# Rotary embedding: the halves of each head exchanged by transfers in SBUF instead of permutation products

## The chip, the cores and the metric

One core of a Trainium2 chip. The metric is the device time of one execution in microseconds; a kernel's time is the median of its runs. TensorE, VectorE, ScalarE and GpSimd run side by side, each with its own stream of instructions, and wait for each other on semaphores; the transfers are issued from SyncE's and ScalarE's streams.

## The reference

One inference step of a two-layer encoder trunk over 512 prompt tokens and 64 sample tokens, handled together as 576 columns. Each layer has three token mixers fed by one projection (an mLSTM with 4 heads of 128, a gated MLP, a sliding-window attention with 8 query heads and 2 key heads of 64), a gated merge, an output projection and a SwiGLU network. The part that matters here is the rotary embedding of the attention's queries and keys:

```python
def rope(x, pos):
    half = x.shape[-1] // 2
    ...
    x1, x2 = xf[..., :half], xf[..., half:]
    return jnp.concatenate([x1 * cos - x2 * sin, x1 * sin + x2 * cos], axis=-1).astype(x.dtype)
```

Every feature of a head needs, beside itself, the feature 32 places on or back in the same head.

## The kernel before

Activations lie with features on the partitions and the 576 tokens along them. Weights stream in chunks of 128 output features (1024 x 128, 512 KB). For each chunk SyncE loads a raw buffer, GpSimd splits it in two operations (L747 makes the high part, L750 the low part, both 128x1024, reading the raw buffer and another tile in SBUF), and TensorE makes 48 products of 288 columns (L799, function `feature_group`, called by `main`). Mostly two pairs of split buffers are in use, so the split of a chunk waits until TensorE has ended the chunk two before it (semaphore chunk_used), and TensorE waits for the split of its own (chunk_split). ScalarE copies each finished chunk out of PSUM (`tile`, L1630).

PSUM is four units of 1024 columns. Every result has its place in one written-out list, `MIX` among others, and takes the unit of its place modulo 4; it waits until the unit's former holder, four places before, has been read (`empty`, `read`).

The order of TensorE's work around the change is written out by hand. The four query chunks wq0 to wq3 (to the tile `wq`) and the chunks su0 to su3 are put between the steps of the mLSTM's heads h = 0 to 3: `scores(h)`, `outputs(h)` and `back(h)` (transposes, L1208 and L1209). The keys' chunk wk went to the tile `kall` (KA is one half of it) long before. Then come su1, back(3), the rotary products of the keys (`rope(4)`) and of query tile 0, su2, those of tiles 1 and 2, su3, that of tile 3, the key transposes ko (L1289, L1290), the chunk sv0, and the first score products of the attention (`sw_scores(0)`, L1308). These wait for all five rotations (rope_ready) and for a copy of the keys with their two heads exchanged (kx_moved), which ScalarE issues as two transfers within SBUF behind the first rotation. Three more chunks sv1 to sv3 alternate with the attention's steps.

A rotary product (L1274) multiplies a tile of 128 features (two heads of 64) by the permutation matrix `perm` from the constants, in two halves of 288 columns, into one PSUM unit r0 to r4. VectorE then rotates: for the keys and the four query tiles in turn, `rope(i)` makes tile x cos, unit x sin, and writes the sum over the tile. All of VectorE's two-operand operations are recorded under L1910. Before this VectorE ends the mLSTM's last head: `gate_head(3)` (L2302), ScalarE's y_hi (L1681), and `y_lo(3)`.

On ScalarE the copies of wq0 to wq3 stand between the heads' steps: `head_hi(h)` writes y_hi, `decay(h)` the exponentials with which VectorE's `weigh_scores(h)` makes the operand of `outputs(h)`. The tile `mid` holds the mLSTM's queries of head h in its slice h and the keys in slice 4 + h; these are last read by the products of `scores(h)`, whose last unit is a3_h. Slices 6 and 7 later take the layer norm's parameters (`LNG`, `LNB`).

Of the kernel before, what the change touches and what calls it, by code (L numbers as in the profile page):

```python
# [16 lines left out]
T = SEQ + DSEQ  # L17
# [20 lines left out]
for _n, _w in (("ident", 128), ("mneg", 128), ("ones", 128), ("perm", 128), ("cos", T),  # L38
               ("sin", T), ("m1", 256), ("sel", 512)):
    CO[_n] = (_at, _at + _w)  # L40
    _at += _w
NCONST, NFIRST = _at, CO["perm"][0]


def constants():
# [3 lines left out]
    def put(n, a):  # L49
        c[:a.shape[0], CO[n][0]:CO[n][1]] = a  # L50
    p = np.arange(128)
    put("ident", np.eye(128, dtype=np.float32))
    swap = np.where(p % 64 < 32, p + 32, p - 32)
    perm = np.zeros((128, 128), np.float32)
    perm[swap, p] = 1.0
    put("perm", perm)
# [87 lines left out]
def swa_slot(i):  # L144
# [8 lines left out]
    + ["r4", "r0", "su2", "r1", "r2", "su3", "r3", "ko"]  # L153
# [131 lines left out]
def build(nc, A, O):  # L285
# [4 lines left out]
    with ctx:  # L290
# [146 lines left out]
        kx_moved, out_done = sem("kx_moved"), sem("out_done")  # L437
        dve_step, act_step = sem("dve_step"), sem("act_step")
# [322 lines left out]
        def _(pe):  # L761
# [15 lines left out]
            for l in range(DEPTH):  # L777
# [483 lines left out]
                def rope(i):  # L1261

                    nm = f"r{i}"
                    pe.wait_ge(unit_of(l, nm), empty(l, nm))
                    if i == 4:
                        if apart(l, "wk", nm):
                            pe.wait_ge(unit_of(l, "wk"), read(l, "wk"))
                        src = KA[:, 0:T]
                    else:
                        if apart(l, f"wq{i}", nm):  # L1270
                            pe.wait_ge(unit_of(l, f"wq{i}"), read(l, f"wq{i}"))
                        src = WQ[:, i, :]
                    for h in range(2):
                        m = pe.matmul(halves(l, nm)[:, h, :], K_["perm"], src[:, h * HALF:(h + 1) * HALF],  # L1274
                                      start=True, stop=True)
                    m.then_inc(done_by(nm), 1)

                main("su1", P_SU + 1)
                back(3)
                rope(4)  # L1280
                rope(0)
                main("su2", P_SU + 2)
                rope(1)
                rope(2)
                main("su3", P_SU + 3)
                rope(3)
# [185 lines left out]
        def _(act):  # L1472
# [19 lines left out]
            for l in range(DEPTH):  # L1492
# [193 lines left out]

                tile("mo0", MO[:, 0, :], ACT.Tanh, 0.5)
# [11 lines left out]
                tile("wq1", WQ[:, 1, :])  # L1699
                head_hi(1)  # L1700
                decay(2)
                tile("wq2", WQ[:, 2, :])
                tile("wq3", WQ[:, 3, :])
                head_hi(2)
                decay(3)
# [4 lines left out]
                act.wait_ge(unit_of(l, _a(3)[2]), read(l, _a(3)[2]))  # L1710
# [894 lines left out]
```

## Time and profile before

| | us |
|---|---|
| median of 3 runs | 2123.87 (2123.57 to 2126.81) |
| the profiled execution | 2126.99 |
| its span, first to last instruction | 2125.2 |
| TensorE busy | 2092.9 (98%) |
| GpSimd busy | 1216.3 (57%) |
| VectorE busy | 696.2 (33%) |
| ScalarE busy | 409.2 (19%) |

Times within the trace are counted from the span's start. Busy time of TensorE includes products that overlap, so the chain of waits, which follows the work back from the end, tells better what an instruction costs on the path. Each product in f32 with plain operands is recorded as two instructions.

### The profile page before, as it was taken

Reading aid. Unit: us, or ns where it says so; the run is one execution under the profiler, and the core shown is the slowest. Engines: PE = TensorE matmul, PEld = TensorE weight load, DVE = VectorE, ACT = ScalarE, POOL = GpSimd, SP = SyncE. Lnnn points to the kernel's source line nnn. Section 1 sums busy time; section 2 is a strip of 40 time slices with the busy share of each in tenths; the row PEclk is TensorE's granted clock in tenths of the full one; section 3 lists DMA queues with packets and bytes.
Section 4 is the critical chain, followed back from the end, with each engine's and each line's share of the span. In section 5 each row is a group of like instructions: output and inputs, shape, how many; then the busy total and the mean of one; then the engine's idle time right before and its main releaser. Section 6 shows DMA issues by size and latency. Waiting matters only on the chain.

```text
span 2125.2 us, 37767 instructions
## 1 busy us (share of the span) xinstructions
PE 2092.9 (98%) x16679; PEld 2021.3 (95%) x16679; DVE 696.2 (33%) x1223; ACT 409.2 (19%) x906; POOL 1216.3 (57%) x596
## 2 busy tenths in 40 slices
PE   7999999999999999999999999999999999999997
PEld 6999898999999999999999989899999999999997
DVE  5223466331345110011464245662315621001113
ACT  4111124111132110011222111431103311111111
POOL 0454454568663666667745445446686366666764
PEclk9999999999999999999999999999999999999999
DMA  9745221223343432332522342223234122222322
GB/s 338 251 144 60 69 72 50 78 75 100 89 159 130 151 115 76 127 89 79 171 61 60 60 70 71 60 60 83 73 107 159 50 70 80 75 85 80 89 69 86
DMA packets 298323, 211.03 MB, mean 99 GB/s; under 512 B 12544, under 2 KB 292656, under 8 KB 294960
## 3 DMA queue, kind: packets, MB, share of 16 engines
q1 hardware_dynamic: 291264, 204.88, 33.3%
q10 hardware_dynamic: 6896, 3.73, 0.8%
q8 instruction: 132, 2.16, 0.4%
q14 instruction: 31, 0.25, 0.0%
HBM read 203.80 MB, written 4.07 MB: 98 GB/s over the span
## 4 chain that ended last, share of the span: by engine, by line
PE 95%; DVE 2%; DMA 1%; POOL 1%; ACT 1%; issue 0%; DVEq 0%; SPq 0%; POOLq 0%
PE ps L799 64%; PE ps L824 13%; PE ps L843 3%; PE ps L849 2%; PE ps L967 1%; PE ps L891 1%; PE ps L1180 1%; PE ps L1345 1%; PE ps L1308 1%; PE ps L1195 1%; PE ps L1323 1%; PE ps L1010 1%; PE ps L870 1%; DMA raw<-in_w_in 1%; PE ps L1375 1%; PE ps L1274 0%
## 5 line engine op out<-in xcount | busy, mean ns | idle before, releaser
L799 PE MATMUL ps<-h_hi,hi_lo 128*128 128x288 f32 x5504 | 977.4, 297 | 1.1 <-issue 0.8
L747 POOL TENSOR_TENSOR hi_lo<-raw,consts 128x1024 fp32r<-128x1024 f32 (+2 forms) x258 | 462.8, 1794 | 768.2 <-PE ps L799 516.9
L799 PEld LDWEIGHTS ps<-h_hi,hi_lo 128*128 128x128 f32 x5504 | 814.7, 189 | 8.5 <-issue 6.1
L750 POOL TENSOR_TENSOR hi_lo<-raw,hi_lo 128x1024 fp32r<-128x1024 f32 (+2 forms) x258 | 599.8, 2325 | 20.2
L799 PE MATMUL ps<-h_lo,hi_lo 128*128 128x288 f32 x2752 | 589.4, 296 | 0.0
L799 PEld LDWEIGHTS ps<-h_lo,hi_lo 128*128 128x128 f32 x2752 | 443.8, 189 | 0.0
L824 PE MATMUL ps<-y_hi,hi_lo 128*128 128x288 f32 x1232 | 220.3, 298 | 0.9 <-POOL hi_lo L750 0.8
L1910 DVE TENSOR_TENSOR tmp<-sq,ps 128x576 f32<-128x576 f32 x44 | 33.2, 755 | 570.7 <-PE ps L799 562.6
L824 PEld LDWEIGHTS ps<-y_hi,hi_lo 128*128 128x128 f32 x1232 | 181.9, 189 | 2.6 <-POOL hi_lo L750 2.0
L824 PE MATMUL ps<-y_lo,hi_lo 128*128 128x288 f32 x616 | 131.7, 295 | 0.0
L1630 ACT ACTIVATE tmp<-ps 128x576 f32<-128x576 f32 x60 | 39.1, 652 | 380.6 <-PE ps L799 380.6
L747 POOL TENSOR_TENSOR hx<-raw,consts 128x1024 fp32r<-128x1024 f32 x28 | 55.0, 1965 | 92.9 <-DVE h_lo L2015 52.9
L799 PE MATMUL ps<-y_hi,hi_lo 128*128 128x288 f32 x576 | 104.5, 298 | 0.0
L824 PEld LDWEIGHTS ps<-y_lo,hi_lo 128*128 128x128 f32 x616 | 99.1, 188 | 0.0
L799 PEld LDWEIGHTS ps<-y_hi,hi_lo 128*128 128x128 f32 x576 | 85.3, 188 | 2.1 <-issue 1.6
L1850 ACT ACTIVATE y_hi<-tmp 128x576 fp32r<-128x576 f32 x44 | 30.2, 686 | 265.5 <-DVE tmp L1910 265.5
L1630 ACT ACTIVATE sq<-ps 128x576 f32<-128x576 f32 x48 | 31.3, 652 | 230.1 <-PE ps L799 224.4
L750 POOL TENSOR_TENSOR lx<-raw,hx 128x1024 fp32r<-128x1024 f32 x28 | 67.0, 2392 | 2.2
L799 PE MATMUL ps<-h_hi,hx 128*128 128x288 f32 x304 | 66.1, 299 | 1.6 <-DVE ps L2049 1.4
L799 PE MATMUL ps<-h_hi,lx 128*128 128x288 f32 x304 | 65.1, 296 | 0.0
L799 PE MATMUL ps<-h_lo,hx 128*128 128x288 f32 x304 | 65.0, 295 | 0.0
L799 PE MATMUL ps<-y_lo,hi_lo 128*128 128x288 f32 x288 | 61.5, 295 | 0.0
(346 smaller groups left out, 2363.5 us busy)
## 6 DMA issues: line engine op xcount, KB each, us to landing
raw<-in_w_in SPq DMA_DIRECT2D x108, 512.0 KB, 3.7
ada<-in_w_ada SPq DMA_DIRECT2D x23, 2048.0 KB, 9.2
raw<-in_w_ffn_in SPq DMA_DIRECT2D x88, 512.0 KB, 3.9
raw<-in_w_ffn_out SPq DMA_DIRECT2D x32, 384.0 KB, 3.4
raw<-in_w_ffn_out SPq DMA_DIRECT2D x32, 320.0 KB
raw<-in_w_out SPq DMA_DIRECT2D x16, 512.0 KB, 4.0
raw<-in_w_br_mlstm SPq DMA_DIRECT2D x8, 512.0 KB, 3.4
raw<-in_w_br_swa SPq DMA_DIRECT2D x8, 512.0 KB, 3.4
```

The costliest lines, as they stand in the source:

```text
L747: pool.tensor_tensor(hi, RAW[s][:, 0:size], ONES[:, 0:1].to_broadcast([128, size]), ALU.mult).then_inc(chunk_hi, 1)
L750: pool.tensor_tensor(lo, RAW[s][:, 0:size], hi.bitcast(f32), ALU.subtract).then_inc(chunk_split, 1)
L799: m = pe.matmul(o[:, h, :], a[:, k, c0:c0 + 128], mv(k, h), start=(k == 0 and begins), stop=(k == nk - 1 and a is wl))
L824: m = pe.matmul(o[:, h, :], a[:, k - k0, :], mv(k, h), start=(k == 0 and begins), stop=(k == nb - 1 and a is wl))
L843: pe.matmul(halves(l, nm)[:, h, :], a[:, k, :], HM[0](k, h), start=(x == 0 and a is wh), stop=False)
L849: m = pe.matmul(halves(l, nm)[:, h, :], wh[:, k, :], HM[1](k, h), start=False, stop=(x == 7))
L870: m = pe.matmul(o, HH[:, h], both[:, :, k, :], start=(k == 0), stop=(k == 7))
L891: m = pe.matmul(unit(l, name)[:, c + t * SUMW:c + (t + 1) * SUMW], sq[:, t0:t0 + 128], ONES[:, 0:SUMW], start=(begins and t == 0), stop=en ...
L967: m = pe.matmul(unit(l, nm)[32 * x:32 * x + 32, 0:128], CS[:, k, :], wv[:, k, x * 128:(x + 1) * 128], start=(k == 0), stop=(k == 7))
L1630: act.activation(split2(dst), halves(l, name), func, scale=scale).then_inc(unit_of(l, name), 1)
L1850: act.activation(y_tile(False, i), TS[:, e, :], ACT.Copy).then_inc(gh_ready, 1)
L1910: return dve.tensor_tensor(out, a, b, op)
```

## The change

The permutation matrix leaves the constants, and the ten rotary products a layer leave TensorE, with their five PSUM units. ScalarE issues, for the keys and each query tile, four transfers of 32 partitions that write the tile with its halves exchanged into the slice `mid[:, i]`: behind wq1's copy for the keys and tile 0, behind wq3's for tile 1, behind head 2's y_hi for tile 2 and behind head 3's y_hi for tile 3, each once a3_h has been read. VectorE multiplies that slice by sin where it multiplied the PSUM unit, and waits for the transfers (half_swapped) where it waited for the product.

```diff
--- before.py
+++ after.py
@@ -35,11 +35,11 @@
 
 CO = {}
 _at = 0
-for _n, _w in (("ident", 128), ("mneg", 128), ("ones", 128), ("perm", 128), ("cos", T),
+for _n, _w in (("ident", 128), ("mneg", 128), ("ones", 128), ("cos", T),
                ("sin", T), ("m1", 256), ("sel", 512)):
     CO[_n] = (_at, _at + _w)
     _at += _w
-NCONST, NFIRST = _at, CO["perm"][0]
+NCONST, NFIRST = _at, CO["cos"][0]
 
 
 def constants():
@@ -50,10 +50,6 @@
         c[:a.shape[0], CO[n][0]:CO[n][1]] = a
     p = np.arange(128)
     put("ident", np.eye(128, dtype=np.float32))
-    swap = np.where(p % 64 < 32, p + 32, p - 32)
-    perm = np.zeros((128, 128), np.float32)
-    perm[swap, p] = 1.0
-    put("perm", perm)
     put("mneg", np.where(p[:, None] <= p[None, :], 0.0, NEG).astype(np.float32))
     put("ones", np.ones((128, 128), np.float32))
     pos = np.concatenate([np.arange(SEQ), PAST + np.arange(DSEQ)]).astype(np.float32)
@@ -150,7 +146,7 @@
 
 MIX += _a(0) + ["mo2"] + _b(0)[0] + ["mo3"] + _b(0)[1] + _a(1) + ["wq0"] + _b(1)[0] + ["wq1"] + _b(1)[1] \
     + _a(2) + ["wq2"] + _b(2)[0] + ["wq3"] + _b(2)[1] + _a(3) + ["su0"] + _b(3)[0] + ["su1"] + _b(3)[1] \
-    + ["r4", "r0", "su2", "r1", "r2", "su3", "r3", "ko"]
+    + ["su2", "su3", "ko"]
 for _i in range(4):
     MIX += [f"sv{_i}"] + ([f"svt{_i - 1}"] if _i else []) + swa_slot(_i)
 BRANCHES = (("ml", 0, 0), ("sw", 2, 1), ("sg", 1, 0))
@@ -435,6 +431,7 @@
             "part_done", "part_staged", "part_back", "part_read"))
         vrow_loaded = sem("vrow_loaded")
         kx_moved, out_done = sem("kx_moved"), sem("out_done")
+        half_swapped = [sem(f"half_swapped{i}") for i in range(5)]
         dve_step, act_step = sem("dve_step"), sem("act_step")
         init_done, cs_ready, x_in_t, x_out_added = (sem(n) for n in (
             "init_done", "cs_ready", "x_in_t", "x_out_added"))
@@ -1258,32 +1255,10 @@
                 main("su0", P_SU)
                 outputs(3)
 
-                def rope(i):
-
-                    nm = f"r{i}"
-                    pe.wait_ge(unit_of(l, nm), empty(l, nm))
-                    if i == 4:
-                        if apart(l, "wk", nm):
-                            pe.wait_ge(unit_of(l, "wk"), read(l, "wk"))
-                        src = KA[:, 0:T]
-                    else:
-                        if apart(l, f"wq{i}", nm):
-                            pe.wait_ge(unit_of(l, f"wq{i}"), read(l, f"wq{i}"))
-                        src = WQ[:, i, :]
-                    for h in range(2):
-                        m = pe.matmul(halves(l, nm)[:, h, :], K_["perm"], src[:, h * HALF:(h + 1) * HALF],
-                                      start=True, stop=True)
-                    m.then_inc(done_by(nm), 1)
-
                 main("su1", P_SU + 1)
                 back(3)
-                rope(4)
-                rope(0)
                 main("su2", P_SU + 2)
-                rope(1)
-                rope(2)
                 main("su3", P_SU + 3)
-                rope(3)
                 pe.wait_ge(unit_of(l, "ko"), empty(l, "ko"))
                 pe.wait_ge(rope_ready, nth(rope_ready, l, 0))
                 pe.transpose(unit(l, "ko")[:, 0:128], KA[:, SEQ - 128:SEQ], IDN)
@@ -1684,6 +1659,15 @@
                     act.wait_ge(unit_of(l, _b(h)[1][0]), read(l, _b(h)[1][0]))
                     y_hi(h, YT[:, :])
 
+                def swap_halves(i, h):
+
+                    src, nm = (KA, "wk") if i == 4 else (WQ[:, i, :], f"wq{i}")
+                    act.wait_ge(unit_of(l, nm), read(l, nm))
+                    act.wait_ge(unit_of(l, _a(h)[2]), read(l, _a(h)[2]))
+                    for a in range(0, 128, 32):
+                        b = a + 32 if a % 64 == 0 else a - 32
+                        act.dma_start(MID[a:a + 32, i, :], src[b:b + 32, 0:T]).then_inc(half_swapped[i], 16)
+
                 tile("mo0", MO[:, 0, :], ACT.Tanh, 0.5)
                 store_state(0)
                 store_state(1)
@@ -1697,17 +1681,21 @@
                 decay(1)
                 tile("wq0", WQ[:, 0, :])
                 tile("wq1", WQ[:, 1, :])
+                swap_halves(4, 0)
+                swap_halves(0, 0)
                 head_hi(1)
                 decay(2)
                 tile("wq2", WQ[:, 2, :])
                 tile("wq3", WQ[:, 3, :])
+                swap_halves(1, 1)
                 head_hi(2)
+                swap_halves(2, 2)
                 decay(3)
                 tile("su0", SU[:, 0, :])
                 tile("su1", SU[:, 1, :])
                 head_hi(3)
 
-                act.wait_ge(unit_of(l, _a(3)[2]), read(l, _a(3)[2]))
+                swap_halves(3, 3)
                 for dst, nm in ((LNG, "ln_v_g"), (LNB, "ln_v_b")):
                     act.dma_start(dst, row(nm).to_broadcast([128, 512])).then_inc(ln_loaded, 16)
 
@@ -2321,14 +2309,12 @@
                     dve.wait_ge(tables_loaded, 16)
 
                 def rope(i):
-                    nm = f"r{i}"
                     raw = KA[:, 0:T] if i == 4 else WQ[:, i, :]
                     dve.wait_ge(unit_of(l, "wk" if i == 4 else f"wq{i}"), read(l, "wk" if i == 4 else f"wq{i}"))
                     tt(TS[:, 0, :], raw, K_["cos"], ALU.mult).then_inc(dve_step, step())
-                    dve.wait_ge(done_by(nm), done(l, nm))
-                    tt(split2(TS[:, 1, :]), halves(l, nm), split2(K_["sin"]), ALU.mult).then_inc(unit_of(l, nm), 1)
+                    dve.wait_ge(half_swapped[i], 64 * (l + 1))
+                    tt(TS[:, 1, :], MID[:, i, :], K_["sin"], ALU.mult).then_inc(dve_step, step())
                     dve.wait_ge(dve_step, step.all())
-                    dve.wait_ge(unit_of(l, nm), read(l, nm))
                     tt(raw, TS[:, 0, :], TS[:, 1, :], ALU.add).then_inc(rope_ready, 1)
 
                 for j, i in enumerate((4, 0, 1, 2, 3)):
```

**TensorE's order.** From the last head's back transposes to the key transposes, before (the products of su2 and su3 left out; L1274 are the rotary products):

```order
L1209 MATMUL ps<-consts,kw 128x64
L1274 MATMUL ps<-kall,consts 128x288 [waits unit_free1,unit_free0]
L1274 MATMUL ps<-kall,consts 128x288
L1274 MATMUL ps<-wq,consts 128x288 [waits unit_free2,unit_free1]
L1274 MATMUL ps<-wq,consts 128x288
...
L1274 MATMUL ps<-wq,consts 128x288 [waits unit_free0,unit_free3]
L1274 MATMUL ps<-wq,consts 128x288
L1274 MATMUL ps<-wq,consts 128x288 [waits unit_free1,unit_free0]
L1274 MATMUL ps<-wq,consts 128x288
...
L1274 MATMUL ps<-wq,consts 128x288 [waits unit_free3,unit_free2]
L1274 MATMUL ps<-wq,consts 128x288
L1289 MATMUL ps<-consts,kall 128x128 [waits rope_ready,unit_free3]
```

And now (L1206 is the back transpose, L796 a chunk's product, L1264 the key transposes, L1283 the first score products):

```order
L1206 MATMUL ps<-consts,kw 128x64
L796 MATMUL ps<-h_hi,hi_lo 128x288 [waits unit_free0,chunk_split]
...
L1264 MATMUL ps<-consts,kall 128x128 [waits rope_ready,unit_free2]
L1265 MATMUL ps<-consts,kall 64x128
...
L1283 MATMUL ps<-kall,wq 128x128 [waits kx_moved,rope_ready,unit_free0]
L1283 MATMUL ps<-kall,wq 128x128 x3
```

The ten rotary products are gone; su2 stands right behind the back transposes, and the waits of the key transposes and of the score products are for the same things as before.

**VectorE's order**, from the last y_lo through the rotation of the keys to the first product of tile 1, before:

```order
L1910 TENSOR_TENSOR y_lo<-ytmp,y_hi 128x576 [waits yh_ready]
L1910 TENSOR_TENSOR tmp<-kall,consts 128x576 [waits unit_free1,tables_loaded]
L1910 TENSOR_TENSOR tmp<-ps,consts 128x576 [waits group_done]
L1910 TENSOR_TENSOR kall<-tmp 128x576 [waits unit_free0,dve_step]
L1910 TENSOR_TENSOR tmp<-wq,consts 128x576 [waits unit_free2,rope_ready]
L1910 TENSOR_TENSOR tmp<-ps,consts 128x576 [waits group_done]
L1910 TENSOR_TENSOR wq<-tmp 128x576 [waits unit_free1,dve_step]
L1910 TENSOR_TENSOR tmp<-wq,consts 128x576 [waits unit_free0,rope_ready]
```

And now:

```order
L1898 TENSOR_TENSOR y_lo<-ytmp,y_hi 128x576 [waits yh_ready]
L1898 TENSOR_TENSOR tmp<-kall,consts 128x576 [waits unit_free1,tables_loaded]
L1898 TENSOR_TENSOR tmp<-mid,consts 128x576 [waits half_swapped4]
L1898 TENSOR_TENSOR kall<-tmp 128x576 [waits dve_step]
L1898 TENSOR_TENSOR tmp<-wq,consts 128x576 [waits unit_free2,rope_ready]
L1898 TENSOR_TENSOR tmp<-mid,consts 128x576 [waits half_swapped0]
L1898 TENSOR_TENSOR wq<-tmp 128x576 [waits dve_step]
L1898 TENSOR_TENSOR tmp<-wq,consts 128x576 [waits unit_free0,rope_ready]
```

The operations are as many and in the same order; the product with sin has `mid` in place of `ps`, and waits for a transfer.

**ScalarE's order**, from the copies of wq0 and wq1 and from those of wq2 and wq3, before:

```order
L1630 ACTIVATE wq<-ps 128x576 [waits chunk_used] x2
L1681 ACTIVATE y_hi<-ytmp 128x576 [waits unit_free1]
L1670 ACTIVATE wdecay<-ps,a_cols 128x384 [waits d_ready]
...
L1630 ACTIVATE wq<-ps 128x576 [waits chunk_used] x2
L1681 ACTIVATE y_hi<-ytmp 128x576 [waits unit_free0]
L1670 ACTIVATE wdecay<-ps,a_cols 128x384 [waits d_ready]
```

And now:

```order
L1605 ACTIVATE wq<-ps 128x576 [waits chunk_used] x2
L1669 DMA mid<-kall 32x576 [waits unit_free2,unit_free1]
L1669 DMA mid<-kall 32x576 x3
L1669 DMA mid<-wq 32x576 [waits unit_free2]
L1669 DMA mid<-wq 32x576 x3
L1656 ACTIVATE y_hi<-ytmp 128x576 [waits unit_free1]
...
L1605 ACTIVATE wq<-ps 128x576 [waits chunk_used] x2
L1669 DMA mid<-wq 32x576 [waits unit_free1,unit_free0]
L1669 DMA mid<-wq 32x576 x3
L1656 ACTIVATE y_hi<-ytmp 128x576 [waits unit_free0]
L1669 DMA mid<-wq 32x576 [waits unit_free0,unit_free1]
L1669 DMA mid<-wq 32x576 x3
```

Eight issues stand ahead of one y_hi, four ahead of the next and four behind it. Behind the last of these four the decay exponentials follow. In GpSimd's and SyncE's orders no row has moved; SyncE's load of the constants is 128 columns shorter.

## Rows read from the trace of the kernel before

**Rows 1.** The page: busy times; the chain that ended last, by engine
```profile
PE 2092.9 (98%) x16679; PEld 2021.3 (95%) x16679; DVE 696.2 (33%) x1223; ACT 409.2 (19%) x906; POOL 1216.3 (57%) x596
...
PE 95%; DVE 2%; DMA 1%; POOL 1%; ACT 1%; issue 0%; DVEq 0%; SPq 0%; POOLq 0%
```

**Rows 2.** The chain in order of time: start us, us, what
```profile
132.61 8.09 PE ps L799 x48
...
228.06 2.23 PE ps L1195 x20
...
258.91 2.14 PE ps L1274 x8
...
267.43 1.94 PE ps L1274 x8
...
275.75 0.97 PE ps L1274 x4
...
283.32 0.65 PE ps L1308 x8
```

**Rows 3.** VectorE's timeline, first layer: start us, us, instruction [idle before]
```profile
223.97 0.21 DVE L2268 SCALAR_TENSOR_TENSOR wdecay<-ps,wdecay 64x64 f32<-64x64 f32 x1
...
263.31 0.75 DVE L1910 TENSOR_TENSOR tmp<-kall,consts 128x576 f32<-128x576 f32 x1
263.98 0.75 DVE L1910 TENSOR_TENSOR tmp<-ps,consts 128x576 f32<-128x576 f32 x1
264.83 0.76 DVE L1910 TENSOR_TENSOR kall<-tmp 128x576 f32<-128x576 f32 x1
...
267.15 0.76 DVE L1910 TENSOR_TENSOR wq<-tmp 128x576 f32<-128x576 f32 x1
267.94 2.33 DVE L1910 TENSOR_TENSOR tmp<-wq,consts 128x576 f32<-128x576 f32 x1
270.20 0.74 DVE L1910 TENSOR_TENSOR tmp<-ps,consts 128x576 f32<-128x576 f32 x1
271.05 2.10 DVE L1910 TENSOR_TENSOR wq<-tmp 128x576 f32<-128x576 f32 x1
...
277.62 1.02 DVE L1910 TENSOR_TENSOR wq<-tmp 128x576 f32<-128x576 f32 x1
```

**Rows 4.** GpSimd's timeline, same stretch and columns
```profile
267.57 2.09 POOL L747 TENSOR_TENSOR hi_lo<-raw,consts 128x1024 fp32r<-128x1024 f32 x1 [4.80 <-PE ps L799]
269.74 2.79 POOL L750 TENSOR_TENSOR hi_lo<-raw,hi_lo 128x1024 fp32r<-128x1024 f32 x1
```

**Rows 5.** ScalarE's timeline and its queue's issues (ACTq), same columns
```profile
168.88 0.45 ACTq L1658 DMA_DIRECT2D out_C_sample<-c_out  x1
169.37 3.87 ACTq L1660 DMA_DIRECT2D out_n_sample<-c_out  x1
...
216.97 0.65 ACT L1630 ACTIVATE wq<-ps 128x576 f32<-128x576 f32 x1 [8.89 <-PE ps L799]
218.46 0.68 ACT L1681 ACTIVATE y_hi<-ytmp 128x576 fp32r<-128x576 f32 x1 [0.83 <-DVE ytmp L2302]
219.86 1.21 ACT L1670 ACTIVATE wdecay<-ps,a_cols 128x384 f32<-128x384 f32 x3 [0.72 <-DVE dmask L1910]
```

**Rows 6.** The tile kall, written by transfers within SBUF
```profile
DMA to landing us min/median/max: 2.7/2.8/2.8
```

**Rows 7.** Two stretches (busy by engine, PEclk is the granted clock); TensorE's last work
```profile
core 0: us, PE busy (x) PEld busy (x) DVE busy (x) ACT busy (x) POOL busy (x), PEclk, DMA share, GB/s
133.50:136.90 3.40, 3.40 (x16) 3.40 (x15) 0.00 (x0) 0.00 (x0) 1.78 (x1) 0.50 0.12 23
2120.00:2125.00 5.00, 0.00 (x0) 0.00 (x0) 1.84 (x2) 0.00 (x0) 0.00 (x0) 0.50 0.84 295
...
2114.71 0.71 PE L950 MATMUL ps<-consts,mid 128*128 128x128 f32 x5
```

## The prediction

> **What bounds the kernel now.** I read the profile's page first: TensorE is busy for 98% of the span and the chain of waits lies on it for 95% [rows 1]. So what leaves TensorE's stream shortens the run, as long as TensorE then waits for nothing new. The second view is the chain in order of time around the rotary products. It gives what they cost on the path: 2.14 us for those of the keys and of query tile 0, 1.94 us for tiles 1 and 2, and 0.97 us up to the key transposes for tile 3 [rows 2]. The third is VectorE's timeline over the same stretch: it works through the five rotations from 263.31 to 278.64, while TensorE asks for the last of them (semaphore rope_ready) only at its first score products, 283.32 [rows 2, 3]. The rotation is therefore hidden by 4.7 us, and that cover is what the change draws on. GpSimd's timeline, laid beside it, tells what stretches VectorE's operations [rows 4]. The second layer repeats the stretch.
>
> **TensorE: taken off.** Ten rotary products per layer go, 2.14 + 1.94 + 0.97 = 5.05 us, all on the path; two layers make 10.1 us. The score products would then come up at 283.32 - 5.05 = 278.27. On the way su2's group of 48 ends at 267.43 - 2.14 = 265.29 and su3's at 275.75 - 2.14 - 1.94 = 271.67. Five fewer PSUM units are used, which turns the rotation of the four banks but leaves each later unit behind the same predecessor, except ko, sv0, sc0 and sv1, whose predecessors (su1, the last head's back transposes, su2, su3) are read soon after they are made.
>
> **ScalarE: added.** 20 transfers a layer are issued in its stream. An issue occupies its queue for 0.45 us in a long burst [rows 5]. Eight stand between wq1 and head 1's y_hi: from 216.97 they run to about 220.6, where y_hi started at 218.46 and the decay exponentials at 219.86 [rows 5]. The decay is then 1.4 us or so late, and the weighted scores, ready at 223.97 + 0.21 = 224.18 [rows 3], come at 225.6; TensorE asks for them at 228.06 [rows 2]. Hidden, with 2.5 us to spare. Query tiles 1 and 2 delay the next decay by less than 1 us in the same place of the next head. The last four issues, behind the last y_hi, are over by about 261.7; a transfer within SBUF lands in 2.8 us [rows 6], so the last half is there by 264.5, long before its product. ScalarE's later waits (the key transfers, su2, the stores of k and v) are short of work as before. I cost the transfers at nothing; their cover is ScalarE's idle time, and if it were gone the price is in rival 3. The bytes are few: five tiles of 128x576 f32, 1.5 MB a layer, as much as three chunks of weights.
>
> **VectorE: changed.** It has as many operations as before, but the product with sin now reads the tile mid and the table, both in SBUF, where it read PSUM and the table. The rows show what that means. A product from PSUM that began at 270.20 took 0.74 us although GpSimd was at work from 269.74 to 272.53; the operations with two SBUF inputs at 267.94 and 271.05 took 2.33 and 2.10 us and ended 0.61 and 0.62 us after GpSimd's operation did [rows 3, 4]. No row has a product of mid, so its price lies between 0.75 us, free, and a whole wait for GpSimd's operation, up to 2.4 us more. I take the second: its nearest rows are the products with cos, same form, same engine, both inputs in SBUF. The Trainium skill, page "SBUF — State Buffer", section "Who interferes with whom", says the same of the unseen case: an operation with two SBUF inputs contends with a GpSimd operation that reads SBUF and is wholly blocked, one with a single SBUF input is not. By that rule, and the rows at 267.94, 270.20 and 271.05 agree with it, the time is the forecast below; if the added product were exempt, it would be rival 1's.
>
> So I work the five rotations through by four rules from the rows. (a) Left alone, cos and sin products follow each other by 0.67 us, the sum starts 0.1 us behind and ends 0.76 us later; a rotation takes 2.31 us. (b) An operation that asks while GpSimd works ends 0.62 us after GpSimd. (c) Between GpSimd's two operations of a split one of VectorE gets in; the first (hi) ends 1.75 us after the VectorE operation it waited for (267.91, 269.66), the second (lo) 2.26 us after (270.27, 272.53). (d) A split is asked for 0.14 us after TensorE ends the chunk two before [rows 2, 3, 4].
> - Keys: 263.31 to 265.59, free.
> - The split behind su2 is asked for at 265.43: hi to 267.34, cos of tile 0 to 267.96, lo to 270.21, sin to 270.83, sum 270.93 to 271.69.
> - cos of tile 1 to 272.47. The split behind su3 (asked 271.81): hi to 274.21, sin to 274.83, lo to 277.08, sum to 277.70.
> - cos of tile 2 to 278.48. The split behind sv0 (asked 278.41): hi to 280.22, sin to 280.84, lo to 283.09, sum to 283.71.
> - Tile 3 is free, since GpSimd now waits for TensorE: 283.74 to 286.02.
>
> I also tried the ties the other way round (at 265.6, 271.8 and 278.4): the end moves between 285.9 and 286.4, since it is mostly set by GpSimd's third split. GpSimd itself is late for no one: lo ends at 270.21 for a chunk needed at 271.8, at 277.08 for one needed behind the scores.
>
> **The new wait.** TensorE stands at the first score products from 278.27 to about 286.14 (0.12 us for the semaphore), 7.87 us. It held 4.7 us of slack, lost 5.05 and saw the rotations end 7.4 us later. Net per layer 7.87 - 5.05 = 2.82 us. Queued behind it are sv1, the transposes and the attention's slots; the softmax of slot 0 is then free of GpSimd and not late.
>
> **The clock.** TensorE ended its last work at 2115.42, and over 2120 to 2125 its granted clock was 0.50, the lower level (1.2 GHz): an idle stretch of 4.6 us was enough [rows 7]. It was 0.50 also from 133.5 to 136.9 [rows 7], with TensorE at work; the chunk in which that lay took 8.09 us on the path, where su2's took 6.38 (from 258.91 + 2.14 = 261.05 to 267.43) [rows 2]. So such a low stretch costs 1.7 us. A wait of 7.87 us is longer than 4.6, so I expect one fall in each layer, reaching into sv1: 1.7 us each.
>
> **Sum.** -10.1 + 2 x 7.87 + 2 x 1.7 = +9.0 us. The profiled execution's 2126.99 (span 2125.2 and 1.8 around it) becomes 2136.0. It lies 3.1 us above the median of the three runs; on the median's scale, 2123.87 + 9.0 = 2132.9.
>
> **Rivals.**
> 1. The added product isn't blocked. The chain of rotations then meets GpSimd as often as before and ends near 278.2, TensorE doesn't wait, and all 10.1 us are kept: 2113.8, faster. It decides wherever VectorE is held up for less than 283.2 - 274.9 = 8.3 us a layer (five free rotations from 263.31 end at 274.9); I forecast 11.1 us, the rows of before have some 3.2. For it: no row shows the case. Against it: the products with cos. Chance 0.12.
> 2. The wait is there, the fall of the clock isn't, or it is over before work resumes: 2 x 2.82 = 5.6, 2129.5. For it: the low at 133.5 was over after 3.4 us, less than the wait. Against it: there TensorE was at work, which it isn't here, and 7.87 is far over 4.6. Chance 0.15.
> 3. ScalarE's queue fills. One issue of the stores took 3.87 us [rows 5]. Were one of the eight to do so, the scores of head 2 would be ready at 225.6 + 3.4 = 229.0 and TensorE 0.9 us late, 1.8 in all: 2134.7. Those stores have 128 pieces of 4 B each, the new ones 32 of 2.3 KB. Chance 0.05.
> 4. VectorE gets two operations in between GpSimd's, or GpSimd's are shorter beside it, so that about half the wait goes: -10.1 + 8 + a fall or none, 2122 to 2126, no change. Chance 0.12.
>
> **Chances.** The forecast itself has 0.56. A measurement of this kernel can tell about 0.2%, 4.2 us, from no change. Faster: rival 1 and a tail of 4, 0.13. Same: most of 4 and a little of 2, 0.13. Slower: the rest, 0.74. The likeliest case alone spans 2130 to 2137 (a fall that costs nothing in one layer, or one twice as long in both). The range leaves out rival 1 and the far tails: 2123.5 to 2137.5.
>
> **What would show it.** Right: no rotary products on TensorE; products tmp<-mid on VectorE with a mean well over 0.75 us; the last sum of the rotations ending about 27 us behind the last back transposes (258.91) and not 20; a wait of TensorE for that sum of 7 to 8 us, twice; granted clock 0.5 in short stretches behind it; ScalarE's decay 1 to 2 us later with no one waiting. Wrong: products of mid at 0.75 us beside a working GpSimd, or no wait of TensorE there.

## The result and the profile after

| | before | after |
|---|---|---|
| median of 5 runs, same chip | 2125.41 us (2123.57 to 2127.05) | 2136.02 us (2134.81 to 2136.85) |
| the profiled execution | 2126.99 | 2136.02 |
| its span | 2125.2 | 2134.2 |
| mean granted clock of TensorE | 0.996 | 0.993 |

The changed kernel is slower: the ratio of the times is 1.0047, with a 95% interval of 1.0036 to 1.0058, which is 7.7 to 12.3 us. The two spans differ by 9.0 us, the sum of the prediction to the tenth. That the last tenth fits is luck, as the account below shows.

The page of the changed kernel, busy times and the chain by engine, to be read against [rows 1]:

```profile
PE 2088.6 (98%) x16639; PEld 2020.1 (95%) x16639; DVE 703.3 (33%) x1223; ACT 409.1 (19%) x906; POOL 1216.4 (57%) x596
...
PE 96%; DVE 2%; issue 1%; ACT 1%; POOL 0%; DMA 0%; DVEq 0%; POOLq 0%; ACTq 0%
```

TensorE has 40 recorded instructions fewer: twenty rotary products, recorded as two each. VectorE is busy for 7.1 us longer with the same number of operations, and "issue" has come up to 1% of the chain. TensorE's waits name the place. Columns: us in total, times, longest.

```profile
PE ps L1283 <- issue: 14.5, 2, 7.3
```

L1283 are the first score products (L1308 before). "issue" means that no event in the trace ended the wait. VectorE's timeline, below, does: the last sum ends at 285.08 and the scores start at 285.18. The other thing that the scores wait for, the exchanged copy of the keys (kx_moved), was issued at 264.95 and 265.81, and no such transfer took more than 4.8 us to land, so it was there long before. The chain in order of time, first layer and then the second (start us, us, what), to be read against [rows 2]:

```profile
258.31 12.98 PE ps L796 x96
...
277.90 7.28 issue
285.18 1.23 PE ps L1283 x8
286.40 8.11 PE ps L796 x48
...
1321.79 7.27 issue
1329.05 1.23 PE ps L1283 x8
1330.28 8.36 PE ps L796 x48
```

No rotary product is left between the chunks. TensorE reaches the scores at 277.90 (the whole layer stands 0.6 us earlier than before: the back transposes end at 258.31 where they ended at 258.91; so the forecast's 278.27 is 277.67 on this scale) and stands for 7.28 us. VectorE's timeline of the same stretch (start us, us, instruction), the rows that answer to [rows 3]:

```profile
262.71 0.74 DVE L1898 TENSOR_TENSOR tmp<-kall,consts 128x576 f32<-128x576 f32 x1
...
265.63 2.45 DVE L1898 TENSOR_TENSOR tmp<-mid,consts 128x576 f32<-128x576 f32 x1
268.11 2.83 DVE L1898 TENSOR_TENSOR wq<-tmp 128x576 f32<-128x576 f32 x1
...
271.66 2.45 DVE L1898 TENSOR_TENSOR tmp<-mid,consts 128x576 f32<-128x576 f32 x1
274.14 2.83 DVE L1898 TENSOR_TENSOR wq<-tmp 128x576 f32<-128x576 f32 x1
...
278.47 2.33 DVE L1898 TENSOR_TENSOR wq<-tmp 128x576 f32<-128x576 f32 x1
280.84 2.78 DVE L1898 TENSOR_TENSOR tmp<-wq,consts 128x576 f32<-128x576 f32 x1
...
284.32 0.76 DVE L1898 TENSOR_TENSOR wq<-tmp 128x576 f32<-128x576 f32 x1
```

GpSimd's timeline beside it, to be read against [rows 4]:

```profile
265.04 2.43 POOL L744 TENSOR_TENSOR hi_lo<-raw,consts 128x1024 fp32r<-128x1024 f32 x1 [2.86 <-PE ps L796]
267.54 2.79 POOL L747 TENSOR_TENSOR hi_lo<-raw,hi_lo 128x1024 fp32r<-128x1024 f32 x1
271.44 2.06 POOL L744 TENSOR_TENSOR hi_lo<-raw,consts 128x1024 fp32r<-128x1024 f32 x1 [1.10 <-PE ps L796]
273.57 2.79 POOL L747 TENSOR_TENSOR hi_lo<-raw,hi_lo 128x1024 fp32r<-128x1024 f32 x1
278.05 2.14 POOL L744 TENSOR_TENSOR hi_lo<-raw,consts 128x1024 fp32r<-128x1024 f32 x1 [1.69 <-PE ps L796]
280.27 2.73 POOL L747 TENSOR_TENSOR hi_lo<-raw,hi_lo 128x1024 fp32r<-128x1024 f32 x1
```

Three splits now fall into the rotations, and each holds up two of VectorE's operations of two inputs in SBUF, every one of which ends 0.61 to 0.62 us after the GpSimd operation beside it (268.08 after 267.47, 270.94 after 270.33). With 0.75 us taken off each product with sin and 0.76 off each other operation, what they take when free, the six are held up for 1.70 + 2.07 + 1.70 + 2.07 + 1.57 + 2.02 = 11.1 us. The rotations take 285.08 - 262.71 = 22.4 us, where they took 15.3 before.

The granted clock in stretches of the first layer (PEclk, 1.00 is 2.4 GHz), where every stretch of before from 272 to 294 shows 1.00:

```profile
core 0: us, PE busy (x) PEld busy (x) DVE busy (x) ACT busy (x) POOL busy (x), PEclk, DMA share, GB/s
...
278.00:285.18 7.18, 0.00 (x1) 0.03 (x1) 7.08 (x6) 0.00 (x0) 4.87 (x2) 0.84 0.35 91
285.20:288.00 2.80, 2.80 (x15) 2.58 (x16) 1.69 (x5) 0.00 (x0) 0.00 (x0) 0.50 0.58 170
288.00:294.00 6.00, 6.00 (x41) 6.00 (x41) 1.38 (x6) 2.28 (x10) 0.00 (x0) 0.85 0.03 7
```

The clock fell to its lower level (0.50, 1.2 GHz) during the wait and was still there when the scores began, with sv1 partly under it. The second layer reads the same (0.50 from 1329 to 1332, 0.81 from there to 1338).

Last, ScalarE's timeline behind wq1's copy (ACTq is an issue of transfers), against [rows 5]:

```profile
216.44 2.53 ACTq L1669 DMA_DIRECT2D mid<-kall  x4
219.07 2.47 ACTq L1669 DMA_DIRECT2D mid<-wq  x4
...
222.17 1.19 ACT L1645 ACTIVATE wdecay<-ps,a_cols 128x384 f32<-128x384 f32 x3
```

The new transfers land 2.1 us after their issue at the median, where the copies of the keys took 2.8 [rows 6]. Eight issues take 5.1 us, and the decay starts 2.9 us later than before (219.86 - 0.60 = 219.26 on this scale). Nobody waits for it: the list of TensorE's waits has no entry for the weighted scores.

**The account**, both layers, from the chains of waits:

| | first layer | second layer | forecast |
|---|---|---|---|
| back transposes to scores, before | 24.41 | 24.40 | |
| the same, after | 26.87 | 26.85 | |
| difference | +2.46 | +2.45 | +2.82 |
| scores and sv1, before | 7.24 | 7.24 | |
| scores and sv1, after | 9.34 | 9.59 | |
| difference | +2.10 | +2.35 | +1.7 |

Together 4.56 and 4.80, 9.4 us. Less the 0.6 us by which the first layer's stretch begins earlier, and with 0.2 us in small differences elsewhere, that is the 9.0 us of the spans. Those 0.6 us are no effect of the change that any run shows: executions differ by more than that ahead of the stretch, as the next section says.

### The profile page after: what moved, and what is told of

The parts are those of the page before. It is cut to its first block, busy times and chain, and to the rows that moved or that the text cites. A ratio compares the mean times of both kernels' runs of the same rounds, so it can differ in the third digit from the quotient of the medians.

```text
span 2134.2 us, 37718 instructions
## 1 busy us (share of the span) xinstructions
PE 2088.6 (98%) x16639; PEld 2020.1 (95%) x16639; DVE 703.3 (33%) x1223; ACT 409.1 (19%) x906; POOL 1216.4 (57%) x596
## 4 chain that ended last, share of the span: by engine, by line
PE 96%; DVE 2%; issue 1%; ACT 1%; POOL 0%; DMA 0%; DVEq 0%; POOLq 0%; ACTq 0%
PE ps L796 65%; PE ps L821 13%; PE ps L840 3%; PE ps L846 2%; PE ps L964 2%; PE ps L888 1%; PE ps L1177 1%; PE ps L1320 1%; PE ps L1283 1%; PE ps L1192 1%; PE ps L1298 1%; PE ps L1007 1%; PE ps L867 1%; PE ps L1350 1%; PE ps L1169 0%
## 5 line engine op out<-in xcount | busy, mean ns | idle before, releaser
L796 PE MATMUL ps<-h_hi,hi_lo 128*128 128x288 f32 x5504 | 980.1, 298 | 0.2 <-ACT kall L1605 0.2
L796 PEld LDWEIGHTS ps<-h_hi,hi_lo 128*128 128x128 f32 x5504 | 818.1, 190 | 7.4 <-issue 5.7
L796 PE MATMUL ps<-h_lo,hi_lo 128*128 128x288 f32 x2752 | 591.1, 297 | 0.0
L796 PEld LDWEIGHTS ps<-h_lo,hi_lo 128*128 128x128 f32 x2752 | 445.6, 190 | 0.0
L796 PE MATMUL ps<-y_hi,hi_lo 128*128 128x288 f32 x576 | 104.5, 298 | 0.0
L796 PEld LDWEIGHTS ps<-y_hi,hi_lo 128*128 128x128 f32 x576 | 85.3, 188 | 2.1 <-issue 1.6
L796 PE MATMUL ps<-h_hi,hx 128*128 128x288 f32 x304 | 66.2, 299 | 1.6 <-DVE ps L2037 1.4
L796 PE MATMUL ps<-h_hi,lx 128*128 128x288 f32 x304 | 65.1, 296 | 0.0
L796 PE MATMUL ps<-h_lo,hx 128*128 128x288 f32 x304 | 65.0, 296 | 0.0
L796 PE MATMUL ps<-y_lo,hi_lo 128*128 128x288 f32 x288 | 61.5, 295 | 0.0
```

The source lines that it names most:

```text
L796: m = pe.matmul(o[:, h, :], a[:, k, c0:c0 + 128], mv(k, h), start=(k == 0 and begins), stop=(k == nk - 1 and a is wl))
```

## The experiments

Two readings stood against each other. The first, *cover and phase*: TensorE comes 5 us earlier, which uses up the cover and moves the splits against the rotations, so that GpSimd holds VectorE up more. The second, *the added block*: what lengthens the rotations is that the product with sin has lost its input in PSUM, and that alone. Beside them, the price of the clock. Each kernel's ratio is to the kernel before, run beside it; that one's median was 2127.53 us beside e1 to e4 and 2127.93 us beside e5 to e8 (2125.41 beside the changed kernel). All spans below are those of profiled executions. Ahead of the stretch in question executions differ: the back transposes end between 257.3 and 260.2 us, and the chunk near 132 us took 8.1 us in some kernels' profiles and 6.6 in others'. So the stretch's own rows are read first, and the ratio second.

### e1: PSUM read kept, product of one column, no transfers

From the kernel before, the rotary products cut to one column:

```diff
-                    for h in range(2):
-                        m = pe.matmul(halves(l, nm)[:, h, :], K_["perm"], src[:, h * HALF:(h + 1) * HALF],
-                                      start=True, stop=True)
-                    m.then_inc(done_by(nm), 1)
+                    pe.matmul(unit(l, nm)[:, 0:1], K_["perm"], src[:, 0:1], start=True, stop=True).then_inc(done_by(nm), 1)
```

> The kernel before, with each rotary product cut from 576 columns to one, so TensorE loses nearly all of the 5.05 us a layer, while VectorE still reads PSUM for the product with sin; no transfers. Left out: the exchange of halves (the PSUM units hold older contents), so queries and keys are rotated wrongly. Theory 'added block' (what the record's rival 1 assumed): without the added SBUF reads the rotations end near where they ended before, TensorE waits for nothing, and the time is about 9 us below before (about 2116). Theory 'phase' (formed on reading the result): the chunks of GpSimd come earlier against the rotations, and the ten operations that were always open to blocking are held more often; worked through by the rules of the record the last sum ends about 20.7 us behind the keys' first product (15.3 before, 22.4 in the changed kernel), TensorE waits some 5 us, the clock falls, and the time is 0 to 5 us above before.

Measured: 2122.11 us, ratio 0.9978 [0.9969, 0.9986]. Neither theory's time came. Since the units r0 to r4 were left in the rotation of PSUM, TensorE waited for VectorE in another place. The chain, start us, us, what:

```profile
272.80 1.44 DVE tmp L1907 x2
274.24 0.14 issue
274.38 6.63 PE ps L799 x48
```

The chunk sv0 waits for a unit whose former holder VectorE has just read. TensorE so reaches the scores at 281.00, the splits come later than in the changed kernel (265.69, 273.57 and 281.15), and the rotations take 17.6 us, 262.92 to 280.49. No wait stands before the scores. The edit changed what it was to hold fixed, so the run can't price the added input; e7 was made for that. It does show two things. Of the products' 10.1 us only 4.7 came home, in part because TensorE waited four times for such units, 3.0 us in all over both layers. And the rotations took 2.2 us longer than before (17.57 for 15.33) with no input added, by the new places of the splits alone.

### e2: the transfers and the product of mid, the rotary products kept

From the kernel before: ScalarE's issues and VectorE's product as in the changed kernel; the rotary products stay and their result isn't read.

```diff
+                swap_halves(4, 0)
+                swap_halves(0, 0)
 ...
                     dve.wait_ge(done_by(nm), done(l, nm))
-                    tt(split2(TS[:, 1, :]), halves(l, nm), split2(K_["sin"]), ALU.mult).then_inc(unit_of(l, nm), 1)
+                    dve.wait_ge(half_swapped[i], 64 * (l + 1))
+                    tt(TS[:, 1, :], MID[:, i, :], K_["sin"], ALU.mult).then_inc(unit_of(l, nm), 1)
```

> The kernel before with the changed kernel's transfers and VectorE's product with sin from SBUF, but TensorE's ten rotary products a layer kept (results unused). The added blocking and the transfers are both in; TensorE's earliness is not. Theory 'cover': by the record's rules the rotations end about 19.1 us behind the keys' first product, 1 us before TensorE asks; no wait, the same time as before (within 1.5 us). Rival 'transfers cost' (late landings, ScalarE's issues delaying the heads): the time is above before by most of the 10 us of the changed kernel though no product was taken off. Rival 'added block alone is enough': TensorE waits at the first scores by 2 us or more a layer, time 4 us or more above before.

Measured: 2128.89 us, ratio 1.0007 [0.9998, 1.0016]. VectorE's timeline, and the chain at the scores:

```profile
277.36 2.94 DVE L1924 TENSOR_TENSOR tmp<-mid,consts 128x576 f32<-128x576 f32 x1
...
280.40 0.76 DVE L1924 TENSOR_TENSOR wq<-tmp 128x576 f32<-128x576 f32 x1
```
```profile
282.05 0.65 PE ps L1309 x8
```

The product of mid is held up twice (the other time, from 268.93 on, for 2.95 us), and the rotations take 19.1 us and not 15.3. But they end at 281.16, 0.9 us ahead of the scores. The path from the back transposes to the scores is 24.41 us, as before (257.64 to 282.05). So the added input and the 20 issues a layer cost nothing as long as the products are there as cover. The 3.8 us by which the input lengthens the rotations here are paid for only once the path is shorter; of the issues and transfers no run shows a price, in either case.

### e3: six other products in the wait

From the changed kernel: ahead of TensorE's wait, six products of 384 columns whose result nobody reads.

```diff
                     if i == 0:
+                        for _ in range(6):
+                            pe.matmul(unit(l, nm)[:, 0:384], IDN, CST[:, 0:384], start=True, stop=True)
                         pe.wait_ge(rope_ready, nth(rope_ready, l, 4))
```

> The changed kernel with six idle products of 384 columns (results overwritten) ahead of the first scores, where TensorE stands idle for 7.3 us a layer. The wait stays as long, but TensorE is at work for some 6.4 us of it. Theory 'clock': the granted clock doesn't fall there, the scores take 0.65 and the chunk sv1 6.59 us again instead of 1.23 and 8.1 to 8.4, and the time is 4.0 to 4.6 us below the changed kernel (about 2131.5). Rival: the slow scores and sv1 have another cause (the start behind a wait, VectorE or ScalarE late), and the time stays at 2136.

Measured: 2131.89 us, ratio 1.0028 [1.0019, 1.0037], 4.0 us below the changed kernel by the two ratios. TensorE's timeline of the first layer, then the chain, sv1 of the first layer and scores and sv1 of the second:

```profile
276.68 4.03 PE L1276 MATMUL ps<-consts 128*128 128x384 f32 x12
284.08 0.72 PE L1285 MATMUL ps<-kall,wq 64*128 64x128 f32 x8 [3.37 <-DVE wq L1900]
```
```profile
284.79 6.59 PE ps L796 x48
...
1325.71 0.71 PE ps L1285 x8
1326.42 8.10 PE ps L796 x48
```

The filling took 4.0 us and not the 6.4 meant, so 3.4 us of idle time were left. In the first layer the clock stayed at 1.00 (284 to 294) and sv1 took 6.59 us; in the second it fell within sv1, which took 8.10 us. From the end of sv0 to the end of sv1 the first layer takes 14.54 us (276.84 to 291.38) against 16.61, the second 16.03 against 16.85. Those 2.1 and 0.8 us are what the filling gave back with the rotations as slow as in the changed kernel. The spans differ by 4.3 us; 1.1 us of the rest lies before the first rotation (261.65 against 262.71) and has nothing to do with the filling. Where the clock stayed up, scores and sv1 took 7.3 us and not 9.3 beside a last sum that came as late as ever: that 2.0 us is the clock's share, seen apart from the wait.

### e4, e5, e6: rotations put into VectorE's idle time

From the changed kernel. All five, the first two or the first one of the rotations (keys, then query tiles) are made between the mLSTM's heads, once their tile is there; tile 3 goes to slice 5 of mid, and each set of transfers is issued once its tile has been copied. For e4:

```diff
+EARLY = {0: (4,), 1: (0, 1), 2: (2, 3)}
+SWAP_AT = (0, 1, 2, 5, 4)
 ...
                         weigh_scores(h + 1)
+                        for i in EARLY.get(h, ()):
+                            rope(i)
```

The other two differ in EARLY alone: e5 moves the keys and tile 0 (`{0: (4,), 1: (0,)}`), e6 the keys alone (`{0: (4,)}`).

> The changed kernel with the five rotations moved into VectorE's idle stretches between the mLSTM's heads (the keys behind head 1's weighted scores, query tiles 0 and 1 behind head 2's, 2 and 3 behind head 3's); the transfers issued earlier, tile 3's halves in another free slice of mid. Nothing is left out. Theory: the only loss was the wait for the rotations and the clock behind it; without it the full 10.1 us of products come home: 2115.3, TensorE's wait at the first scores gone, no granted clock of 0.5 there. Rival 'ScalarE or the heads' chain': transfers and rotations amid the heads make the normalising or the decay late, TensorE waits at the outputs or the back transposes, and 2 to 8 us of the gain are lost (2117 to 2123).

Measured: 2116.54 us, ratio 0.9947 [0.9935, 0.996]. The chain, first layer:

```profile
259.49 12.98 PE ps L798 x96
...
272.68 6.39 PE ps L798 x48
279.08 0.65 PE ps L1285 x8
```

No wait, no fall of the clock; the path from the back transposes to the scores is 19.59 us where it was 24.41. Two layers give 9.6 us, inside the interval of the ratio (8.5 to 13.8 us). As many transfers and issues as in the changed kernel and the product of mid are still there, at earlier places. This version beats both kernels.

> As the kernel with all rotations early, but only the keys' and query tile 0's are moved; tiles 1 to 3 stay where they were. By the record's rules tile 1 runs free, tiles 2 and 3 take 6.0 us each, and the last sum ends at about 277, 0.9 us before TensorE asks: no wait, the whole gain (2115 to 2117), the same as with all five moved. If anything else than the count of rotations left held TensorE (transfers, the key copy), it would wait here too.

Measured: 2116.95 us, ratio 0.9946 [0.9933, 0.9959]. VectorE's last sum, and the chain at the scores:

```profile
276.01 2.83 DVE L1901 TENSOR_TENSOR wq<-tmp 128x576 f32<-128x576 f32 x1
```
```profile
279.77 0.65 PE ps L1285 x8
```

Two of five are enough: the last sum ends at 278.84, 0.9 us ahead, though each of the two remaining splits still holds VectorE up. More slack than that earns nothing, as e4 shows.

Early transfers have a price of their own, which this profile shows. The keys' halves are now issued behind the mLSTM's state stores, where the DMA engines were already busy before the change (share 0.92 from 180 to 190). Issued from 188.53 on, they had landed only when VectorE's product began:

```profile
210.67 0.76 DVE L1901 TENSOR_TENSOR tmp<-mid,consts 128x576 f32<-128x576 f32 x1 [6.65 <-DMA mid<-kall]
```

VectorE came late to the next head's work, and TensorE waited 0.7 us for it there. The median from issue to landing of these eight transfers is 10.3, 15.1 and 12.6 us in e4, e5 and e6, against 2.1 where the changed kernel issues them. In the profiles of e4 and e6 no wait of TensorE came of it.

> As the one before, but only the keys' rotation is moved. Tile 3's rotation then meets the third split: by the record's rules the last sum ends at about 280.8, 2.9 to 3.1 us after TensorE asks. 6 us of the gain are lost, and with a fall of the clock behind the wait up to 4.4 more: 2121 to 2126. Rival: the wait is proportional to the rotations left (four fifths of 7.3 us), about 2129.

Measured: 2125.54 us, ratio 0.9988 [0.9979, 0.9997]. The chain in the first and the second layer:

```profile
278.86 3.01 issue
...
282.59 6.58 PE ps L798 x48
...
1316.89 2.99 issue
...
1320.60 8.10 PE ps L798 x48
```

One rotation takes 4.3 us off the wait, not the 2.24 us that it takes by itself. The other 2.0 us are a hold that is gone: in the changed kernel the third split held up a sum and the last tile's product with cos, here only the last sum (279.44, 2.33 us), since no rotation is left behind it. In the first layer the clock stayed up and sv1 took 6.58 us, in the second 8.10. The wait of 3.01 us is the one that was expected, and not the 5.8 us of the rival: the time does not go down in proportion to the work moved.

### e7: the product of mid without its second input in SBUF

From the changed kernel, since e1 had not told:

```diff
-                    tt(TS[:, 1, :], MID[:, i, :], K_["sin"], ALU.mult).then_inc(dve_step, step())
+                    dve.tensor_reduce(MX[:, 0, 0, :], MID[:, i, :].rearrange("p (a c) -> p a c", a=4), AX.X,
+                                      ALU.max).then_inc(dve_step, step())
```

> The changed kernel with each product of mid and sin replaced by a maximum over mid: one SBUF input, about the same length, so never open to GpSimd's hold; everything else as changed. Left out: the sine part of the rotation, so queries and keys are rotated wrongly. Theory 'added block': the added second SBUF input is what makes the rotations late; without it TensorE doesn't wait and about 10 us come home (2115 to 2117). Theory 'phase': the ten operations open to blocking before are now met by GpSimd's earlier splits in the worst order; worked through by the record's rules the rotations still end about 20.9 us behind the keys' first product (22.4 in the changed kernel), TensorE waits 5.8 instead of 7.3 us, and the time is some 3 us below the changed kernel (about 2133).

Measured: 2131.27 us, ratio 1.0012 [1.0003, 1.0021]. VectorE's timeline and the chain:

```profile
279.86 0.74 DVE L2316 TENSOR_REDUCE mx<-mid 128x4 f32<-128x576 f32 x1
280.64 2.12 DVE L1898 TENSOR_TENSOR wq<-tmp 128x576 f32<-128x576 f32 x1
```
```profile
277.21 5.65 issue
```

GpSimd was at work from 279.40 to 282.13. The reduction, of one input in SBUF, took 0.74 us beside it, and the sum behind it, of two, ended 0.63 us after it. The wait of TensorE is 5.65 us: taking the second input away takes 1.6 of its 7.28 us, no more, and the rotations still need 20.7 us (262.03 to 282.76). An operation that isn't held up only hands its place to the next one, which is. The rest is cover and phase. The input has no fixed price: beside the splits of before it makes the rotations 3.8 us longer (e2, 19.1 for 15.3), beside those of the changed kernel 1.6 us (22.4 for 20.7). The two shorter waits and the clock behind them account for 3.3 us; the two spans differ by 4.7, the ratios by 7.4 with some 3 us of uncertainty, and the rest lies outside this stretch. On the one point of the forecast that rested on the Trainium skill ("SBUF — State Buffer", "Who interferes with whom") the trace agrees with the rule on both sides: two inputs in SBUF blocked, one not.

### e8: the third split held back until the rotations are over

From the changed kernel, GpSimd alone:

```diff
+                    if pos == P_SV + 2:
+                        pool.wait_ge(rope_ready, nth(rope_ready, l, 4))
```

> The changed kernel, but GpSimd waits for the last rotation before it splits the chunk sv2 (the split that meets the rotations of tiles 2 and 3). Nothing is left out. If GpSimd's hold on the shared port is what stretches the rotations: tiles 2 and 3 take 2.3 us each, the last sum ends 3.5 us earlier, TensorE waits 3.7 instead of 7.3 us, 7 us or more come home (2129), and up to 4.4 us more if the granted clock doesn't fall behind so short a wait (2124.5). Rival: the split is itself late for TensorE's chunk sv2 and takes the gain back (2133 to 2136).

Measured: 2126.49 us, ratio 0.9994 [0.9985, 1.0003]. The chain, first layer, and GpSimd's split:

```profile
277.62 3.70 issue
281.32 1.06 PE ps L1285 x8
282.38 7.76 PE ps L798 x48
```
```profile
281.35 1.89 POOL L746 TENSOR_TENSOR hi_lo<-raw,consts 128x1024 fp32r<-128x1024 f32 x1 [5.26 <-DVE wq L1900]
```

With the third split out of the way, tiles 2 and 3 run free (276.75 to 281.22) and the wait falls from 7.28 to 3.70 us, as expected. So 3.6 us of the wait are the third split's, and one added wait in GpSimd's stream takes back all of the loss, though it wins none of the gain of e4. The late split itself is late for no one: it ends at 285.70, and its chunk begins at 291.77. The clock fell in both layers even after the shorter wait, and it fell late: in the first layer it was 1.00 all through the wait (277.7 to 281.3), 0.57 from 281.3 to 283 and 0.51 to 285, with TensorE at work again.

## Why the prediction was right, and where it wasn't

- **What leaves TensorE.** Forecast 5.05 us a layer, measured 24.41 - 19.59 = 4.82: su2 and su3 now run as one piece of 12.98 us, where the two took 6.38 each, 12.76. That much, 0.2 us, of the products' time on the path comes back in the chunks.
- **VectorE held up by GpSimd.** Forecast 11.1 us, measured 11.1. The rules (b) and (c) held on every row. Two things differ: the sum starts 0.03 us behind the product and not 0.1, since no PSUM unit has to be handed back (a free rotation is 2.24 us, not 2.31; e2, which reads mid but still hands the unit back, has the 0.1), and the first tie, at 265, went to VectorE, so that the first split held up sin and sum of tile 0 and not cos and sin. The last sum ended at 285.08 where 286.02 - 0.60 = 285.42 was forecast.
- **The new wait.** Forecast 7.87, measured 7.28 and 7.27: 0.34 us is the earlier last sum, 0.23 the later arrival of TensorE. Where it is gone (e4, e5), with the rest of the change kept at earlier places, the whole gain is there: the wait and its clock are all that turns the gain into a loss.
- **The clock.** The mechanism came in both layers; the term was too small, 1.7 against 2.1 and 2.35, since the row that it was taken from had only a chunk under the low clock and not the score products as well (1.23 us where they take 0.65, 0.6 us of the term). The comparison was off too: the chunk at 132.61 takes 6.58 us where the clock stays up (e2, e7, e8), not su2's 6.38, so its low stretch cost 1.5 us and not 1.7; sv1 lost 1.5 and 1.8. Over both layers the clock came out 1.05 us dearer than forecast and the wait with its products 0.73 us cheaper. The 0.3 us that are left over, the 0.2 us elsewhere and the 0.6 us by which the stretch happened to begin earlier cancel to a tenth. That is why the sum fits to the tenth, and it is luck.
- **ScalarE.** The issue was mis-sized, 0.45 us forecast and 0.61 to 0.62 measured, so the decay is 2.9 us late and not 1.4. The term stays at nothing, but nearer its edge than the prediction said: the weighted scores are ready at 226.47 and TensorE asks for them at 227.46, 1.0 us to spare and not 2.5. None of the new issues took several us, as rival 3 had it. The transfers landed in time wherever the changed kernel issues them; placed earlier they are slow (e5).
- **The rivals.** Rival 2 (no fall) lost in the changed kernel. So did rival 4: GpSimd let one operation of VectorE in between its two each time, and its operations were no shorter. Rival 1 was wrong in itself, beyond its premise. It said that, with the added product exempt, the rotations would meet GpSimd as often as before and end near 278.2, for 2113.8 us. e7 exempts the product, and TensorE still waits for 5.65 us. The hold there is 0.91 + 2.08 + 1.53 + 2.07 + 1.57 + 1.36 = 9.5 us, above the 8.3 from which the rival itself decides. That bound was too wide besides: 283.2 - 274.9 is measured to TensorE's old arrival, so up to 8.3 us the kernel is merely no slower but for the clock; for no wait at all, which the rival claims, the hold must stay below about 278.2 - 274.9 = 3.3 us. Its step "as often as before" was never worked through the rules: with the products gone the splits come at 265, 271 and 278 in place of 267.6 and 275.9. The prediction put the whole question on the added input, whose removal takes off 1.6 us of 7.3.
- **Size against the medians.** The difference of the medians is 10.6 us and that of the spans 9.0; the interval of 7.7 to 12.3 holds both. The absolute median lies 3.1 us above the forecast, 1.5 of which is the kernel before, at 2125.41 in these five runs and 2123.87 in the three shown.

What stays open: e7 and e8 take 1.6 and 3.6 us off the wait one at a time. They weren't tried together, so whether the two add up isn't known, and how the rest of the wait divides between the 5.05 us of lost cover, the first two splits' new places and their ties is argued from rows, not shown. Why the clock fell in one layer and not in the other after nearly the same wait is open too.

## What to carry to other kernels

Work taken off the bottleneck engine is also taken out of the cover of every side chain that it used to wait for, and it shifts the other engines against each other: work the side chain through again at its new times, for the case that seems harmless too. If the side chain becomes late, look for idle time of its engine further up before giving up the change: here moving two of five rotations up turned +10 into -11 us. A wait on TensorE costs more than its length when the granted clock falls in it or behind it. And what is moved up must bring its inputs along in time: look at what the DMA engines do where its transfers will now be issued.

## What the runs showed of the hardware

- The clock did not answer the same wait the same way. Waits of 7.3 and 5.65 us were followed by 0.50 in every layer (the changed kernel and e7). After idle stretches of 3.0 us (e6), 3.4 (e3) and 3.7 us (e8) the next chunk took 6.58 to 6.59 us in two of the six layers and 7.76 to 8.10 in four; in e6 and e3 the two layers of one execution differ. So a wait of 3.0 to 3.7 us cost nothing beyond itself or some 1.5 us more. And the fall came behind such a wait, not in it: in e6's second layer the clock was 1.00 from 1317 to 1319.8, with TensorE idle, 0.91 to 1322 and 0.50 from 1322 to 1325, with TensorE at work.
- Issuing a transfer of 32 partitions x 576 f32 within SBUF holds ScalarE's queue for 0.61 to 0.62 us, four of them 2.5 us, where the small stores of before took 0.45 [rows 5]. How soon it lands depends on the place: 2.1 us at the median in the changed kernel, 10 to 15 us behind the state stores (e4 to e6).
- Exempting one operation from GpSimd's block saved less than its own holds (in e7 1.6 us a layer, where the product with sin had been held up for 2 x 1.70), since the operation behind it ran into GpSimd's work instead.
